# Last down projection in weight pieces of 4 k-tiles by 512 columns, and a region of SBUF that begins on a multiple of 128 bytes

## The reference, cut to what matters

```python
for layer in range(DEPTH):                      # DEPTH = 2, x is (1, 512, 1024)
    h = rms_norm(x, norm_mix_pre[layer])
    m = even_mixer(h, ...) if layer % 2 == 0 else odd_mixer(h, ...)
    x = x + rms_norm(m, norm_mix_post[layer])
    h = rms_norm(x, norm_ffn_pre[layer])
    f = conv_ffn(h, ffn_w_up[layer], ffn_conv_w[layer], ffn_conv_b[layer], ffn_w_down[layer])
    x = x + rms_norm(f, norm_ffn_post[layer])

def conv_ffn(h, w_up, conv_w, conv_b, w_down):
    u = causal_dwconv(h @ w_up, conv_w, conv_b)  # 2 * 2816 columns
    g, val = u[..., :D_FF], u[..., D_FF:]
    return (jax.nn.gelu(g, approximate=True) * val) @ w_down   # 2816 -> 1024
```

## Time and profile before

| | |
|---|---|
| median of 3 runs | 1205.63 us (1205.12 to 1209.6) |
| span of the profiled execution | 1207.1 us |
| PE (TensorE matmul) busy | 1170.7 us, 97% of the span |
| DVE (VectorE) busy | 708.3 us, 59% |
| ACT (ScalarE) busy | 482.7 us, 40% |
| DMA, mean of the 16 engines over the last down projection | 24% |

### The profile page before, as it was taken

The page is one execution under the profiler, slowest core; times in us unless marked ns, Lnnn a source line. Parts: engine busy times, 40 slices in busy tenths (PEclk is TensorE's granted clock), DMA queues, the critical chain, the costliest instruction groups (busy, mean ns, idle before and its releaser), DMA issues.

```text
span 1207.1 us, 15133 instructions
## 1 busy us (share of the span) xinstructions
PE 1170.7 (97%) x5964; PEld 975.9 (81%) x5964; DVE 708.3 (59%) x848; ACT 482.7 (40%) x662; POOL 73.6 (6%) x53
## 2 busy tenths in 40 slices
PE   8999999999999999999999998899999999999997
PEld 7778755788888888888888787687788888899997
DVE  4758447248777766652226787438786667762222
ACT  4637357233444443342223318433544344432220
POOL 2000000033000000000111200032000000000000
PEclk9999979998999999999999999999999999999999
DMA  6323200031523332333332451041333233322331
GB/s 208 105 70 105 69 1 1 1 112 29 140 72 102 104 104 84 90 96 96 96 96 71 113 166 49 1 122 36 105 105 102 79 98 104 105 76 82 97 97 71
DMA packets 147478, 104.41 MB, mean 86 GB/s; under 512 B 4642, under 2 KB 144354, under 8 KB 147426
## 3 DMA queue, kind: packets, MB, share of 16 engines
q1 hardware_dynamic: 146466, 102.36, 28.6%
q10 hardware_dynamic: 960, 1.31, 0.5%
HBM read 98.02 MB, written 2.10 MB: 83 GB/s over the span
## 4 chain that ended last, share of the span: by engine, by line
PE 87%; DVE 6%; ACT 4%; issue 1%; DMA 1%; POOL 0%; POOLq 0%; SPq 0%; DVEq 0%; ACTq 0%
PE ps L1241 26%; PE ps L1243 26%; PE ps L1242 25%; PE ps L1417 2%; PE ps L1431 2%; DVE x L1034 2%; PE ps L1310 1%; ACT prob L749 1%; PE ps L1442 1%; ACT hx_hi L633 1%; DVE hx_lo L1038 1%; PE ps L1303 1%; DVE z_s L916 1%; DVE sp_lo L933 1%; PE ps L1315 1%
## 5 line engine op out<-in xcount | busy, mean ns | idle before, releaser
L1241 PE MATMUL ps<-hx_hi,w_hi 128*128 128x512 f32 x912 | 363.5, 399 | 2.8 <-DVE hx_lo L1038 1.9
L1242 PE MATMUL ps<-hx_lo,w_hi 128*128 128x512 f32 x912 | 357.6, 392 | 0.0
L1243 PE MATMUL ps<-hx_hi,w_lo 128*128 128x512 f32 x912 | 357.5, 392 | 0.0
L787 DVE TENSOR_TENSOR w_lo<-w_raw,w_hi 128x2048 fp32r<-128x2048 f32 (+1 forms) x90 | 201.6, 2240 | 170.2 <-ACT w_hi L507 170.2
L507 ACT ACTIVATE w_hi<-w_raw 128x2048 fp32r<-128x2048 f32 (+1 forms) x90 | 168.4, 1871 | 163.2 <-DMA w_raw<-in_ffn_w_down 115.5
L1241 PEld LDWEIGHTS ps<-hx_hi,w_hi 128*128 128x128 f32 x912 | 172.8, 189 | 43.8 <-DVE hx_lo L1038 4.9
L1242 PEld LDWEIGHTS ps<-hx_lo,w_hi 128*128 128x128 f32 x912 | 172.9, 190 | 37.0 <-issue 1.9
L1243 PEld LDWEIGHTS ps<-hx_hi,w_lo 128*128 128x128 f32 x912 | 172.6, 189 | 36.6
L1241 PE MATMUL ps<-w_hi,g_hi 128*128 128x256 f32 x352 | 99.4, 282 | 0.0
L1243 PE MATMUL ps<-w_hi,g_lo 128*128 128x256 f32 x352 | 99.1, 281 | 0.0
L1242 PE MATMUL ps<-w_lo,g_hi 128*128 128x256 f32 x352 | 99.1, 281 | 0.0
(11 more groups left out here) (193 smaller groups left out, 1564.6 us busy)
## 6 DMA issues: line engine op xcount, KB each, us to landing
w_raw<-in_ffn_w_up SPq DMA_DIRECT2D x88, 512.0 KB, 5.0
w_raw<-in_ffn_w_down SPq DMA_DIRECT2D x16, 1024.0 KB, 5.2
w_raw<-in_even_w_in SPq DMA_DIRECT2D x8, 1024.0 KB, 5.2
w_raw<-in_ffn_w_down SPq DMA_DIRECT2D x8, 768.0 KB, 4.7
w_raw<-in_odd_w_qkv SPq DMA_DIRECT2D x6, 1024.0 KB, 5.0
w_raw<-in_even_w_out SPq DMA_DIRECT2D x4, 1024.0 KB, 5.4
w_raw<-in_odd_w_o SPq DMA_DIRECT2D x4, 1024.0 KB, 6.0
x_in<-in_x SPq DMA_DIRECT2D x4, 512.0 KB, 6.6
```

The costliest lines, as they stand in the source:

```text
L787: dve.tensor_tensor(w_lo[s][:, 0:k], w_raw[s][:, 0:k], w_hi[s][:, 0:k], ALU.subtract).then_inc(w_lo_done, 1)
L1241: pe.matmul(dst, s_hi, r_hi, start=first, stop=False)
L1242: pe.matmul(dst, s_hi, r_lo, start=False, stop=False)
L1243: return pe.matmul(dst, s_lo, r_hi, start=False, stop=last)
```

## The change

The last down projection (layer 1) gets its own code on every engine. Its pieces are now 4 k-tiles (the last one 2) by 512 columns: `WIDE_K` has six pieces, two column halves, again 12 units. `wide` views a slot of 8 x 2 x 128 elements as 4 rows of 512. Each token tile has a whole PSUM bank, so a half uses four banks and the other half the other four (`WIDE_BANKS`); the transposes of `x` go through two banks that the second half uses later, after the first four pieces of the first half. The tail is done for one token tile at a time instead of two. The number of DMAs is the same; a row of a load is 2048 bytes instead of 1024.

Apart from that, `big0` is rounded up to a multiple of 128 bytes: it moves from 137152 to 137216.

```diff
+WIDE_K = [(0, 4), (4, 8), (8, 12), (12, 16), (16, 20), (20, FT)]
...
+    where[0] = (where[0] + P - 1) // P * P
     big0 = where[0]
...
+    def wide(w):
+
+        return w[:].rearrange("p (k a) b n -> p k (a b n)", a=2)
+
+    WIDE_OLD = (group_of(U_DOWN[1]) - N_IN) % 3
+    WIDE_TURN = [2 * ((WIDE_OLD + 1) % 3), 2 * ((WIDE_OLD + 1) % 3) + 1]
+    WIDE_BANKS = [[2 * WIDE_OLD, 2 * WIDE_OLD + 1, 6, 7],
+                  [2 * ((WIDE_OLD + 2) % 3), 2 * ((WIDE_OLD + 2) % 3) + 1] + WIDE_TURN]
...
+            if layer == 1:
+                for half in range(2):
+                    for c, (k0, k1) in enumerate(WIDE_K):
+                        u = U_DOWN[1] + len(WIDE_K) * half + c
+                        slot_free(u)
+                        src = w_down[k0 * P:k1 * P, T * half:T * half + T].rearrange("(k p) n -> p k n", p=P)
+                        load(u, src, wide(w_raw[u % RING])[:, 0:k1 - k0])
...
+            act.activation(sq[t % 2][:], bank(WIDE_BANKS[half][t]), ACT.Square, accum_out=narrow[:, t, half:half + 1]).then_inc(mtok_sq, 1)
...
+        def token_gains(half, t):
...
+            dve.wait_ge(mtok_sq, TT * half + t + 1)
+            if half == 1:
+                dve.tensor_tensor(narrow[:, t, 2:3], narrow[:, t, 0:1], narrow[:, t, 1:2], ALU.add).then_inc(tok_sum, 1)
+            cols = slice(T * half, T * half + T)
+            dve.tensor_tensor(m_tok[:, t, cols], bank(WIDE_BANKS[half][t]), last_gain[:, cols], ALU.mult).then_inc(mtok_done, 1)
+            if half == 0:
                 return
...
+        def last_down():
+            g_end = group_of(U_DOWN[1])
+            n = len(WIDE_K)
+            for half in range(2):
+                for c, (k0, k1) in enumerate(WIDE_K):
+                    u = U_DOWN[1] + n * half + c
+                    unit_ready(u)
+                    pe.wait_ge(g_ready, FT + k1)
...
+                    r_hi, r_lo = wide(w_hi[u % RING]), wide(w_lo[u % RING])
                     for t in range(TT):
-                        dst = ps[:, T * b0 + 256 * t:T * b0 + 256 * t + 256]
                         tt = slice(P * t, P * t + P)
                         for k in range(k0, k1):
-                            r = [w[u % RING][:, k - k0].rearrange("p b n -> p (b n)") for w in (w_hi, w_lo)]
-                            last = three(dst, g_hi[:, k, tt], g_lo[:, k, tt], r[0], r[1], k == 0 and t % 2 == 0, k == FT - 1 and t % 2 == 1)
-                        if c == 2 and t == 1:
+                            last = three(bank(WIDE_BANKS[half][t]), g_hi[:, k, tt], g_lo[:, k, tt], r_hi[:, k - k0], r_lo[:, k - k0],
+                                         k == 0, k == FT - 1)
+                        if c == n - 1 and t < TT - 1:
                             last.then_inc(mtok_mm, 1)
```

More of the change, by code:

```diff
@@ L676, in ffn_up, with token_squares @@
             act.activation(tile_(g_hi, j), cv[:], ACT.Copy).then_inc(g_hi_done, 1)
[L678 to L683, removed]
+        def token_squares(u, half, t):
+            if t < TT - 1:
+                act.wait_ge(mtok_mm, (TT - 1) * half + t + 1)
             else:
                 act.wait_ge(unit_done, u + 1)
-            for t in (2 * b, 2 * b + 1):
-                c0 = T * group_banks(group_of(u)) + 256 * t
-                act.activation(sq[b][:, 256 * (t % 2):256 * (t % 2) + 256], ps[:, c0:c0 + 256], ACT.Square, accum_out=narrow[:, t, mp:mp + 1]).then_inc(mtok_sq, 1)
+            if TT * half + t >= 2:
+                act.wait_ge(mtok_sq, TT * half + t - 1)
+            act.activation(sq[t % 2][:], bank(WIDE_BANKS[half][t]), ACT.Square, accum_out=narrow[:, t, half:half + 1]).then_inc(mtok_sq, 1)
         def ffn(layer):
@@ L697, in ffn @@
                 ffn_up(layer, j, U_UP[layer] + j)
+            if layer == 1:
+                last_down()
+                return
             for mp in range(4):
                 for c in range(3):
-                    u = U_DOWN[layer] + 3 * mp + c
+                    u = U_DOWN[0] + 3 * mp + c
                     v = u + 2
-                    if v < U_DOWN[layer] + N_DOWN:
+                    if v < U_DOWN[0] + N_DOWN:
                         k0, k1 = DOWN_K[(3 * mp + c + 2) % 3]
                         split_hi(v, k1 - k0)
-                    elif v < N_UNITS and c < 2:
+                    elif c < 2:
                         split_hi(v)
@@ L710, in ffn @@
                         for b in range(2):
-                            if b and mp == 3 and v < N_UNITS:
+                            if b and mp == 3:
                                 split_hi(v)
[L713 to L723, removed]
+                            m_squares(3, u, mp, b)
+        def last_down():
+            n = len(WIDE_K)
+            for half in range(2):
+                for c in range(n):
+                    u = U_DOWN[1] + n * half + c
+                    v = u + 2
+                    if v < N_UNITS:
+                        k0, k1 = WIDE_K[(c + 2) % n]
+                        split_hi(v, 2 * (k1 - k0))
+                    if half == 1 and c == 0:
+                        act.preload_act_table_set("sqrt_and_others")
+                    if half == 0 and c < n - 2:
+                        for i in (2 * c, 2 * c + 1):
                             act.wait_ge(xtok_mm, i + 1)
-                            act.activation(x_tok[:, :, P * i:P * i + P], bank(6 + i % 2).rearrange("p (t c) -> p t c", c=P),
+                            act.activation(x_tok[:, :, P * i:P * i + P], bank(WIDE_TURN[i % 2]).rearrange("p (t c) -> p t c", c=P),
                                            ACT.Copy).then_inc(xtok_copied, 1)
+                    if c == n - 1:
+                        for t in range(TT):
+                            token_squares(u, half, t)
+                            if half == 1:
+                                act.wait_ge(tok_sum, t + 1)
+                                act.activation(std[:, t:t + 1], narrow[:, t, 2:3], ACT.Sqrt,
+                                               scale=1.0 / D, bias=eps).then_inc(tok_std, 1)
         out_projection(0, 1)
@@ L1093, in token_gains @@
                 return
[L1094 to L1097, removed]
+            dve.wait_ge(tok_std, t + 1)
+            dve.reciprocal(rcol[:, t:t + 1], std[:, t:t + 1]).then_inc(tok_rms, 1)
+            dve.wait_ge(tok_rms, t + 1)
+            dve.wait_ge(mtok_done, TT + t + 1)
             dve.wait_ge(xtok_copied, DT)
[L1099 to L1103, removed]
+            for h in range(2):
+                part = slice(h * D // 2, (h + 1) * D // 2)
+                dve.scalar_tensor_tensor(out=m_tok[:, t, part], in0=m_tok[:, t, part], scalar=rcol[:, t:t + 1],
+                                         in1=x_tok[:, t, part], op0=ALU.mult, op1=ALU.add).then_inc(out_done, 1)
@@ L1112, in ffn @@
                 ffn_up(layer, j, U_UP[layer] + j)
+            if layer == 1:
+                n = len(WIDE_K)
+                for half in range(2):
+                    for c in range(n):
+                        v = U_DOWN[1] + n * half + c + 2
+                        if v < N_UNITS:
+                            k0, k1 = WIDE_K[(c + 2) % n]
+                            split_lo(v, 2 * (k1 - k0))
+                    for t in range(TT):
+                        token_gains(half, t)
+                return
             for mp in range(4):
                 for c in range(3):
-                    u = U_DOWN[layer] + 3 * mp + c
+                    u = U_DOWN[0] + 3 * mp + c
                     v = u + 2
-                    if v < U_DOWN[layer] + N_DOWN:
+                    if v < U_DOWN[0] + N_DOWN:
                         k0, k1 = DOWN_K[(3 * mp + c + 2) % 3]
                         split_lo(v, k1 - k0)
-                    elif v < N_UNITS and c < 2:
+                    elif c < 2:
                         split_lo(v)
-                    if c == 2 and layer == 0:
+                    if c == 2:
                         m_copy(3, u, mp, group_banks(group_of(u)), between=v if mp == 3 else None)
-                    if c == 2 and layer == 1:
-                        for b in range(2):
-                            token_gains(u, mp, b)
         out_projection(0, 1)
@@ L1505, in ffn @@
                 unit(u0 + j, hx)
-            g_up = group_of(U_DOWN[layer])
+            if layer == 1:
+                last_down()
+                return
+            g_up = group_of(U_DOWN[0])
             for mp in range(4):
                 b0 = group_banks(g_up + mp)
[L1509 to L1512, removed]
+                banks_free(g_up + mp)
                 for c, (k0, k1) in enumerate(DOWN_K):
-                    u = U_DOWN[layer] + 3 * mp + c
+                    u = U_DOWN[0] + 3 * mp + c
@@ L1515, in ffn, with last_down @@
                     unit_ready(u)
[L1516 to L1519, removed]
+                    pe.wait_ge(g_ready, k1)
```

(24 more changed lines are left out.)

13 lines of the change are left out of this document (3 added, 10 removed).

## The result

The changed kernel takes 1210.28 us (median of 8 runs, 1208.14 to 1211.39), the kernel before 1205.38 (8 runs). The ratio is 1.0036, 95% interval 1.0019 to 1.0053: slower by about 4 us, where 6 us less was forecast (1199.5 us, range 1197.0 to 1202.8). The profiled execution's span is 1209.5 us.

A forecast was written before the change was run, and what follows sets the result against it. The prediction took TensorE's own pace to bound the last down projection. Its terms, -4.9 (wide matmuls), -2.0 (region's start), -0.3 (mixers) and +1.1 (tail), gave -6.1 us, so 1205.6 became 1199.5 us, range 1197.0 to 1202.8.

The forecast's parts named there:

- What bounds the kernel, and PE's pace: Last down projection: TensorE's own pace is the bound, PE busy 128.07 of 128.10 us, 118.0 ns per 256-column matmul.
- the four surpluses: TensorE's matmuls: time beyond their columns, 11.1 to 15.6 ns, read from four kinds of operand pairs in the trace.
- The region's start: Layer 0's down projection and the output projections: pitch falls from 228.9 to 226.7 ns, -2.0 us, bounds 0 and -2.0.
- The wide matmuls: Last down projection: 528 matmuls of 512 columns at 226.7 ns replace 1056 at 118.0, -4.9 us (-6.1 to -3.7).
- The tail: After PE's last matmul: VectorE is the bound with four rounds of 2.24 us, +1.1 us, bounds 0 and +3.6.
- Weights in time: Last down projection's weight loads and splits: at least 6.9 us of slack, so the new shape costs nothing.
- The mixers: The mixers' products, which read the same region: -0.3 us taken, bounds 0 and -1.2.
- the parts cancel: Whole change: the wide pitch at which gains and losses balance, put at 237.8 ns.
- The first: Rival, last down projection: surplus stays at 11.2 ns because of `g` itself, pitch 224.5, total 1198.3 us; chance 0.15.
- the second: Rival, region's start: place has no effect, no -2.0 or -0.3, 1201.8 us with pitch 226.7; chance 0.20.
- the third: Rival, after PE's end: each tile's steps run one after another, +3.6 instead of +1.1, 1202.0 us; chance 0.08.
- The fourth: Rival, wide matmuls: surplus goes with each 256 columns, pitch 239.8 ns, 2.0 us more there, total 1206.4; chance 0.05.

The follow-up runs named there:

- base_64: Changed kernel with `where[0] += 192` in place of the rounding and every SBUF buffer 64 bytes further; one execution, pitches 226.7 to 226.9 ns, time not compared.
- wide_only: The changed kernel without the rounding of `big0`, which stays at 137152: 1206.2 us, ratio 1.0002 (0.9985 to 1.0018) to the kernel before.
- align_only: The kernel before with only `big0` rounded up, from 137152 to 137216: 1212.18 us, ratio 1.0065 (1.0041 to 1.0088).
- narrow_192: The kernel before with `where[0] += 192` ahead of `big0`, which then is 137344: 1207.05 us, ratio 1.0006 (0.9989 to 1.0023).

## Why the prediction was wrong

- **What bounds the kernel, and PE's pace**: right. The last down projection is TensorE's pitch times its matmuls, PE without a gap.
- **The step that failed** is the reading of the four surpluses, "hardly depends on the length, and follows where the two operands lie: 2.2 ns more when the moving one is off, 2.1 ns less when the stationary one is", with "off" taken as off a multiple of 128. The rows fitted it, but held only two remainders modulo 128 and did not tell a modulus of 128 from one of 256; weights and `hx` both had 128 modulo 256, and the new start has 0. The runs showed the distance between the two, modulo 256: both off together cost nothing (base_64, 226.7), and the stationary one off by itself costs 6.6 ns at 512 columns (wide_only, 233.3) instead of giving 2.1 back. Nor is the surplus independent of the length: it is 13.2 and 13.4 ns at distance 0, but 11.1 and 20 at 64. With this step two terms were wrong:
  - **The region's start**: -2.0 forecast. With `g` at +4.4 ns and layer 1's and most of layer 0's `y` at +3.5 to +4.4, 528 x 4.4 + 384 x about 3.8 = +3.8 us. The bounds (0 and -2.0) left out the side on which it fell: the text argued that the place might do nothing, never that a place might be worse.
  - **The wide matmuls**: -4.9 forecast. 528 x 0.2324 = 122.7 against 124.6, so -1.9; the bound of 228.9 above ("the highest 512-column pitch") wasn't one, because no row had this distance.
- **The tail**: right, +1.1 forecast, 7.88 against 7.0 = +0.9 measured, and for the reason given: VectorE's rounds run on without a gap, and its last pass ends 5.4 us after PE (5.6 forecast). It is the one term that was worked out from durations of the same instructions.
- **Weights in time**, banks, transposes: right, no wait.
- **The mixers** (-0.3): not separable from the spread of their own time. The part of align_only's time that no pitch here explains may lie in them; that isn't shown.
- **Slips in its sums**, none of which moved the forecast: the parts cancel at a pitch of 238.3 and not 237.8 (125.8 over 528), and with 1.3 us for the wide matmuls the whole would be 2.5 us and not 2.7.
- Sum with the measured terms: +3.8 - 1.9 + 0.9 = +2.8 us, within the measured 1.0019 to 1.0053 (2.3 to 6.4 us), whose middle is 1.5 us higher; that remainder isn't explained.
- **Rivals**: none held. The first (the low surplus is `g`'s own) is refuted by narrow_192, where `g` stationary has 120.0 and not 117.8, and its pitch by wide_only; the second (place does nothing) by align_only; the third (tail in series) by VectorE's rounds. The fourth has the right sign for the whole (slower, 1206.4) by luck: it put the loss into the wide matmuls (239.8), which gained 1.9 us, and kept the gain of the region, where the loss is.

Of the two parts of the change, then, the wide pieces alone are no change that can be told (1.0002), the alignment alone costs 4 us or more (1.0065), and the same wide pieces with the region 128 bytes further on win 0.35%.

## What to carry to other kernels

Where TensorE is the bound, measure its pitch by starts for each pair of operands, note both base addresses, and look at their difference modulo 256 before "aligning" anything: alignment to a round number is no aim in itself, and here moving one region by 64 bytes made 912 matmuls some 4 ns slower each, and moving it by 128 bytes more made them some 6 ns faster. A bound taken from the highest row seen is only a bound if the new case lies among the rows; an address that no row has needs a range on both sides. At a kernel's end, look whether TensorE delivers results faster than the next engine takes them; here, where it did, a long last piece instead of a short one took 2.5 us off the tail.

## What the runs showed of the hardware that was not expected

- The pitch of a 512-column fp32r matmul with a new weight load each time, at a granted clock of 1.00, depends on stationary minus moving address modulo 256: 226.7 ns at 0, 228.9 at 192, 232.4 to 233.3 at 32, 64, 128 and 224. Base addresses are meant; the slices within the buffers lie multiples of 512 bytes apart. Whether the stationary operand of the same matmul counts, or the one that is loaded meanwhile for the next, can't be told here, since both begin at the same remainder.
- It is not symmetric (64 and 192 differ by 4.4 ns), and at 256 columns the order is another: 119.9 at 0, but 117.8 (`g`) and 113.6 (`hx`) at 64 and 118.7 (`g`) at 128. Why, and why the two at 64 differ, is open.
- These pitches are means. Between single starts, `g` moving in the changed kernel goes 229, 238, 229, 238 ns and so on, and the wide stretch repeats every seven matmuls, from 228 to 241, though the operands of a product change in threes; in wide_only every step is 233 or 234. So the distance doesn't fix the single step, and what does is open.
